# A different order of work at the chunk boundary of a DeltaNet and Mamba-2 mixing stage

## What is computed

```python
m = eye + bc[..., :, None] * kk * dec * (1.0 - eye)
u_t = lax.linalg.triangular_solve(m, bc[..., None] * vc, left_side=True, lower=True)
w = lax.linalg.triangular_solve(m, (bc * jnp.exp(gam))[..., None] * kc, left_side=True, lower=True)
...
u = u_c - jnp.einsum('bhcd,bhde->bhce', w_c, s)
o = jnp.einsum('bhcd,bhde->bhce', q_c, s) + jnp.einsum('bhce,bhef->bhcf', qk_c, u)
s = ge[..., None, None] * s + jnp.einsum('bhcd,bhce->bhde', k_c, u)
```

## Time and profile before

| | |
|---|---|
| median of 3 runs | 1929.94 us (1928.34 to 1930.14) |
| the profiled execution | 1928.42 us, its span 1926.6 us |
| mean granted TensorE clock over the span | 0.901 |
| busy over the span: TensorE | 1681.3 us (87%) |
| VectorE | 544.9 us (28%) |
| ScalarE | 402.9 us (21%) |
| GpSimd | 320.9 us (17%) |

### The profile page before, as it was taken

How to read it: one execution, slowest core, us unless ns; L and a number is a source line. 1 busy time by engine, 2 the same in 40 slices (tenths; PEclk the granted TensorE clock), 3 DMA queues, 4 the chain that set the end, 5 groups by cost and what they waited for, 6 DMA issues and landing times. The chain is left out here.

```text
span 1926.6 us, 18077 instructions
## 1 busy us (share of the span) xinstructions
PE 1681.3 (87%) x6288; PEld 1029.6 (53%) x6288; DVE 544.9 (28%) x1113; ACT 402.9 (21%) x988; POOL 320.9 (17%) x253
## 2 busy tenths in 40 slices
PE   8999999995788888898887439999999999999950
PEld 7666666663565776776775224444444444444420
DVE  1345444201434554353552240000000000000007
ACT  1211111112113333444431001111111111111112
POOL 0000000000313433333441000111111111111105
PEclk8999999997559988998888669999999999999985
DMA  6143233224122111222200138999999999999944
GB/s 221 49 121 92 69 82 79 78 60 133 61 87 104 63 43 62 88 88 78 82 34 22 58 120 306 340 340 328 333 333 341 340 328 335 332 340 339 328 117 185
DMA packets 173764, 334.21 MB, mean 173 GB/s; under 512 B 37560, under 2 KB 67176, under 8 KB 172424
## 3 DMA queue, kind: packets, MB, share of 16 engines
q1 hardware_dynamic: 163048, 294.30, 43.8%
q0 software_dynamic: 9504, 34.61, 6.8%
q10 hardware_dynamic: 1152, 4.52, 0.6%
HBM read 281.33 MB, written 52.07 MB: 173 GB/s over the span
## 5 line engine op out<-in xcount | busy, mean ns | idle before, releaser
L1901 PE MATMUL bank<-sb_arena 128*128 128x512 f32 x1024 | 451.7, 594 | 3.6 <-ACT sb_arena L1946 2.5
L358 PE MATMUL bank<-sb_arena 128*128 128x368 f32 x1344 | 421.7, 477 | 6.9 <-DMA sb_arena<-xT 6.9
L358 PEld LDWEIGHTS bank<-sb_arena 128*128 128x128 f32 x1344 | 258.0, 192 | 168.6 <-DMA sb_arena<-w_conv 6.9
L1901 PEld LDWEIGHTS bank<-sb_arena 128*128 128x128 f32 x1024 | 192.8, 191 | 234.4 <-issue 229.9
L1917 PE MATMUL bank<-sb_arena 128*128 128x512 f32 x512 | 227.9, 599 | 8.3 <-DMA sb_arena<-w 8.3
L2000 DVE TENSOR_SCALAR sb_oidx<-sb_slot 128x1 int32 x32 | 4.9, 154 | 548.3 <-DMA d_acc<-sb_arena,sb_oidx 548.3
L1917 PEld LDWEIGHTS bank<-sb_arena 128*128 128x128 f32 x512 | 95.9, 192 | 117.3 <-issue 108.8
L1875 POOL DMA_INDIRECT d_acc<-sb_arena,sb_oidx x32 | 51.0, 1592 | 613.5 <-ACT sb_arena L1964 613.5
L829 PE MATMUL bank<-sb_arena 128*128 128x512 f32 (+1 forms) x288 | 134.0, 606 | 5.7 <-DVE sb_rlog L1388 5.0
L1946 ACT ACTIVATE sb_arena<-bank 128x512 f32<-128x512 f32 x66 | 35.8, 595 | 276.6 <-PE bank L1895 276.6
L1563 POOL TENSOR_TENSOR sb_arena<-sb_arena 128x512 f32<-128x512 f32 (+1 forms) x9 | 11.0, 1222 | 476.4 <-ACT sb_arena L1011 476.4
(11 more groups left out here) (317 smaller groups left out, 1793.7 us busy)
## 6 DMA issues: line engine op xcount, KB each, us to landing
sb_arena<-w SPq DMA_DIRECT2D x192, 1024.0 KB, 7.9
sb_arena<-w_conv SPq DMA_DIRECT2D x28, 512.0 KB, 4.7
d_conv<-sb_arena SPq DMA_DIRECT2D x28, 512.0 KB, 3.2
sb_arena<-d_conv SPq DMA_DIRECT2D x8, 1792.0 KB, 7.7
sb_arena<-d_gam SPq DMA_DIRECT2D x8, 768.0 KB, 4.0
d_x<-sb_arena SPq DMA_DIRECT2D x9, 512.0 KB, 2.6
sb_arena<-xT ACTq DMA_DIRECT2D x8, 552.0 KB, 9.7
sb_arena<-w_out SPq DMA_DIRECT2D x8, 512.0 KB, 4.9
```

Source lines behind the costliest of these rows:

```text
L358: last = e.matmul(bank[3 * r + s][:, 0:TN], wring[n % NV][:, k, :], xT[:, k, TN * s:TN * s + TN], start=(k == 0), stop=(k == KT - 1))
L1901: mm = e.matmul(bank[bk][:], xgT[:, k, :], w[:, k, :], start=(k == 0), stop=(k == KT - 1))
```

## The change

On ScalarE `tokens(i)` is called before `normal(r)`. On VectorE `scores` is cut in two. The mask half (`scores_a`) stays, and `u_scale(p)`, `begin_x` and `shift(r)` come right behind it; `values`, `cb_mask`, `q_recip`, `begin_xt` and the decay half (`scores_b`) follow, all ahead of `s_update(p)`. On GpSimd `level_mask(i, 1)` and `ln_power(r)` are called before `keys(i)`. TensorE's and SyncE's lists are not touched. No instruction is added or removed, and all semaphores and their counts stay.

```diff
@@ -1140,10 +1140,10 @@
                         keys(i)
                     if post and not first:
                         wt_copy(p)
+                    if prep:
+                        tokens(i)
                     if tail:
                         normal(r)
-                    if prep:
-                        tokens(i)
                     if post and not first:
                         o_squares(p)
                     if not prep:
@@ -1261,12 +1261,16 @@
                         e.wait_ge(S["u_ps"], i)
                     e.tensor_tensor(XT[0:n, :, 0:n], idn, bt[0][0:n, :, 0:n], ALU.subtract).then_inc(S["xt0"], 1)
 
-                def scores(i):
+                def scores_a(i):
                     n = n_of(i)
                     e.wait_ge(S["qk_ps"], i + 1)
                     e.wait_ge(S["dm"], i + 1)
                     q_ = qkm[i % 2][0:n, :, 0:n]
                     e.tensor_tensor(q_, heads(ZA)[0:n, :, 0:n], bc1(mk(i)[0:n, INC, 0:n], n, GH, n), ALU.mult).then_inc(S["qkr"], 1)
+
+                def scores_b(i):
+                    n = n_of(i)
+                    q_ = qkm[i % 2][0:n, :, 0:n]
                     e.wait_ge(S["qkr"], i + 1)
                     e.tensor_tensor(q_, q_, dm[0:n, 0:GH, 0:n], ALU.mult).then_inc(S["qkm"], 1)
 
@@ -1408,7 +1412,8 @@
                 lower(0)
                 begin_x(0)
                 begin_xt(0)
-                scores(0)
+                scores_a(0)
+                scores_b(0)
                 values(0)
                 cb_mask(0)
                 q_recip(0)
@@ -1455,17 +1460,19 @@
                     if tail:
                         moments(r)
                     if prep:
-                        scores(i)
-                        values(i)
-                        cb_mask(i)
-                        q_recip(i)
+                        scores_a(i)
                     if post and not first:
                         u_scale(p)
                     if prep:
                         begin_x(i)
-                        begin_xt(i)
                     if tail:
                         shift(r)
+                    if prep:
+                        values(i)
+                        cb_mask(i)
+                        q_recip(i)
+                        begin_xt(i)
+                        scores_b(i)
                     if post and not first:
                         s_update(p)
                     if prep:
@@ -1615,11 +1622,11 @@
                     first = p == 0
                     if prep:
                         k_norm(i)
-                        keys(i)
                         level_mask(i, 1)
                     if tail:
                         ln_power(r)
                     if prep:
+                        keys(i)
                         inputs(i)
                         level_mask(i, 2)
                     if post and not first:
```

## The result

| | before | after |
|---|---|---|
| median | 1929.14 us (4 runs, 1925.81 to 1930.14) | 1885.38 us (4 runs, 1884.70 to 1885.88) |
| ratio, 95% interval | | 0.9776 [0.9759, 0.9793] |
| the profiled execution | 1928.42 us, span 1926.6 | 1884.70 us, span 1882.9 |
| mean granted TensorE clock | 0.901 | 0.912 |

The change makes the kernel 44 us faster. The forecast was 1893, with a range of 1884 to 1908.

The account below looks back on a forecast made before the run. TensorE's stops in the mixing stage were taken as the bound, chiefly o_product waiting for x_tok behind ScalarE's norm. 1928.42 - 38.5 + 2.0 = 1891.9, median 1893 us; own range 1886 to 1900, wider range 1884 to 1908.

Parts of the forecast that it names:

- ScalarE: Tokens ahead of the norm: x_tok is there at 808.1, o_product starts at 808.15, and the 5.0 us stop goes.
- VectorE's queue: VectorE ahead of s_update is late next; second level_y at 818.8, not 825.15; 5.8 us gained, about 1.5 handed back.
- Lost turns: VectorE against GpSimd, ahead of s_update or within cb_decay: 0.3 us lost per chunk, bounds none to 2.3; 5.8 becomes 5.5.
- Level 2 and the clock: Behind level 2: no change taken; bounds 0.8 us less if the clock stays up, 2.0 more if longer case always met.
- Both rivals on the clock: At level 2: clock stays up, 1886.4 us, chance 0.08; or stays down longer, 1907.4 us, chance 0.08.
- The one in which it stays up at level 2: Rival: clock stays up through level 2, 6.5 us gained per chunk in place of 5.5, 1886.4 us; chance 0.08.
- The first chunk: First chunk, without post or tail: GpSimd's queue meets VectorE's products, cbd at 597.7 against 595.7; cost 2.0 us, bounds 0 to 3.
- The sum: Profiled execution: 1928.42 - 38.5 for seven chunks + 2.0 for the first = 1891.9 us; median 1.5 above, said as 1893.

Follow-up runs that it names:

- the executions listed above: Profiled executions of several kernels: first chunk 44.8, 45.4 and 46.1 us with the old VectorE and GpSimd lists in it, 48.2, 49.2, 49.5 and 49.5 with the new.
- two edits that were worth nothing or less alone: Changed kernel with q_norm between o_power and ln_gain (alone 1892.47 us) and router's first transposes behind level 2's second products (alone 1883.85); together 1869.83 us.

## Why the prediction was right, and where its terms were off

*ScalarE.* As predicted: L1036 ends at 791.33, 7.9 us after the chunk's start (predicted 7.9 to 8.0), and L716 follows at 7.97 with no stop. The norm runs behind it and `o_squares` does not wait for it.

*VectorE's queue.* It was named as what is late next, and it is: L1314 no longer waits for L723. The new stop ahead of L772 is 0.47 us where I had 1.4. In my working `s_update` began at 11.9 us after the chunk and `cb_decay` ended at 14.4; in the trace they are at 11.6 and 14.0. `ln_power` took 0.55 us where I had 1.00, so GpSimd's `inputs` were over before `begin_xt` began, and the turn that I had it lose was not lost. With that the second `level_y` is at 18.14 in the mean, 6.3 us earlier, where I worked out 5.8 and took 5.5: 0.5 us is the queue, 0.3 the deduction for lost turns.

*Lost turns.* Off in place, small in size: `begin_xt`, `scores_b` and `cb_decay` lost none in the seven chunks. The one that stood was `shift`, 0.66 us where I had 0.15 (0.49 in one chunk). My deduction of 0.3 us per chunk, for turns lost behind it, had no cause.

*Level 2 and the clock.* Right: from level 2 to level 3 it was 6.42 us in the mean before and is 6.45 after. Both rivals on the clock are out for this kernel. The one in which it stays up at level 2 does exist, in the version without VectorE's part, and in three chunks of the one with ScalarE's part alone even behind a stop of 2.1 us. So the row after one stop of 2.13 us was no proof against it.

*The first chunk.* The step that failed: cost 2.0, bounds 0 to 3, measured 4.3, and 3.6 in the mean of the executions listed above. The turns are much as I had them: L772 starts at 14.09 in place of 12.45, 1.6 us later. What I left out is that TensorE stops 3.4 us for it and the clock falls, and these are the lines:

```profile
591.52 3.19 DVE L1298 TENSOR_TENSOR sb_arena<-sb_arena 128x512 f32<-128x512 f32 x2
...
594.77 3.68 PE L772 MATMUL bank<-sb_arena 128*128 128x64 f32 x16 [3.41 <-DVE sb_arena L1298]
598.24 2.02 PE L732 MATMUL bank<-sb_arena 128*128 128x128 f32 x8
```

3.68 for 2.00 and 2.02 for 1.11 are 2.6 us. I had priced the clock in the chunks that lose a stop and not in the one that gets one.

*The sum.* -38.5 + 2.0 was predicted. Measured are -44.0 + 4.3, and -4.1 in stretches that the change does not touch, of which 2.7 are the clock in the sample products. Without those two outer stretches the profiled execution would stand at 1888.7, against 1891.9 predicted.

The median of 1885.38 is 8 us under the forecast. It lies just below the forecast's own 1886 to 1900, and within the wider range only because that was carried down to 1884 for the rival in which the clock stays up, which did not happen. So the route was right and the fit of the number is in part luck: seven chunks better by 5.5 us and outer stretches better by 4.1 outweigh a first chunk worse by 2.3.

*What the prediction did not see* is which part did it. It read VectorE's new order as what brings `u_scale` forward. The runs show that ScalarE's swap alone gives 37 us, and that GpSimd's, by taking away two lost turns, brings `u_scale` forward nearly as well (`o_product` at 8.23 in place of 7.97) and without the first chunk's loss. With both in place VectorE's part costs 8 us. The 1.71 us of L1271 were in the rows, and I used them to price the new order, not to ask whether the old one needed changing.

## What to carry to other kernels

Where an engine is late, look first at how long its instructions take against their like, and only then at their order: two products that were together 1.4 us too long for standing behind another engine were mended by moving two calls on that engine (15 us on top of ScalarE's swap), where reordering VectorE's whole list gave 6. When a stop on TensorE is removed or made, price the clock on both sides of the ledger, for the stop that goes and for each one that comes. And when an edit removes a wait and the time does not follow, read what the same engine waits for next before giving it up. Here the router's transposes could not start before some 21 us after the chunk's start, whatever was gained ahead of them: two edits that were worth nothing or less alone gave 16 us together.

## What the runs showed of the hardware that was not expected

- A stop of 3.3 to 3.7 us on TensorE ahead of `o_product` lowered the clock in four of seven chunks of one execution and not in the other three; stops of 4.5 to 5.0 us in the kernel before lowered it in all seven. Stops of 1.8 to 2.1 us at level 2 did so in all seven chunks before the change, and stops of 2.1 us in only four of seven in the version with ScalarE's part alone, where this row has L732 at full speed:

```profile
753.48 1.13 PE L732 MATMUL bank<-sb_arena 128*128 128x128 f32 x8 [2.12 <-DVE sb_arena L1339]
```

  Two stops of 1.0 us, 3 us apart, left it up in six chunks of seven. The length of the stop alone does not tell what the clock will do.
- GpSimd's power instruction on 4 columns (L1560, 1.01 us) runs beside VectorE's L1330 (0.17 us) without holding it up, where its product over 1024 columns holds the same L1330 for 2.29 us. The Trainium skill (SBUF — State Buffer, "Who interferes with whom") has a VectorE instruction with two SBUF inputs contend with a GpSimd one that reads SBUF, for a lock that one of them holds alone. For this small power instruction the rows show a much shorter hold than its own length. It does wait its turn: where `q_norm` began beside L1222 (L1560 at 803.26 in the changed kernel), it took 1.99 us.
- The same power instruction on one column took 1.00 us in all seven chunks before the change and 0.55 in all seven after it (L1570 before, L1577 after). Why is not shown.
